# Relative-position bias tables: one matmul product for all eight heads, and one DMA that repeats its source rows

## The chip, the cores and the metric

The kernel runs on one core of one Trainium2 chip. The metric is the device time of one execution in microseconds (us). A core has TensorE (matrix products, PE in the profile), VectorE (DVE), ScalarE (ACT), GpSimd (POOL) and SyncE (SP), each with its own stream of instructions; they meet only through semaphores. SP, ACT and POOL also issue DMA transfers, which run on 16 shared DMA engines.

## The reference, cut to what matters

One layer of a hybrid model: an mLSTM branch and a sparse latent attention branch side by side, then a mixture of experts. Only the attention's relative bias is touched by the change:

```python
def _rel_bucket(dist):            # 32 buckets, exact up to 16, logarithmic up to 128
    n = jnp.maximum(dist, 0)
    ...
# rel_bias is [32 buckets, 8 heads]
l_sel = jnp.einsum('bqhr,bqkr->bqhk', ql, c_sel) + \
    rel_bias[_rel_bucket(t[None, :, None] - sel)].transpose(0, 1, 3, 2)
...
p = jax.nn.softmax(...)
```

The bias of a head depends on the distance between query and key alone. So one row of 656 numbers per head (`FX`), the bias at every distance, holds all that the attention needs; the row of each query is that row shifted by one place.

## The kernel before

The kernel is written by hand, engine by engine, with a semaphore for every hand-over. Input channels are projected in "units" of 256 columns (1024 KB of weights each): SP loads a unit into one of three slots of `raw` (`load(u)`, which waits until VectorE is done with the unit three back), ScalarE rounds it (`split_hi`, L646), VectorE forms the rest (`split_lo`, L1456), and TensorE runs three products per chunk (L1011 to L1013). Two split slots exist, so a split waits for the last use of the unit two back.

The bias goes in four steps. A constant `oneh` [32, 656] says which bucket each distance falls in. TensorE multiplies column h of `relb` [32 buckets, 8 heads], repeated 128 times, by `oneh` (`tables`, L1041): each of 128 partitions of `wide[h % 2]` in PSUM then holds the same 656 numbers of head h. ScalarE copies them to `ftab` [128, 4 buffers, 656] (`tables_out`, L648), and issues a DMA of 328 KB to `table_dram[h]`, shape (8, 128, 656) in DRAM (`tables_store`, L656). Much later SP reads `strips` back with a row step of 655 elements (L424), which shifts each partition's row by one place.

Heads go in pairs. Pair 0 is made before anything else. The others are written into the order of TensorE: `tables(2)` after the first unit's products, `tables(4)` after the second block of unit 1 (`B_QI + 1`), `tables(6)` after the small transposes L1110, then `channel_unit(2)` (two blocks, B_QA), `index_scores(0)`, `channel_unit(3)`, `index_scores(1)`, transposes of `c_tok`, and `conv_unit(4, 0)` to `conv_unit(7, 6)`.

`ftab` lies on the bytes of `v_ext`. For that reason GpSimd waits for all table stores before it writes the ones of `v_ext` (L544), which raises `const_done` to 3; and ScalarE's `conv_in(0)` (L750), which evacuates the first convolution block into `pre`, waits for `const_done` 3. `conv_unit(5, 2)` on TensorE waits for `conv_in(0)`, since it writes the same PSUM. VectorE, from `index_scores(0)` on, runs an order of its own: the score sum, rounds of top-k (L1545, L1546), and between them `split_lo` and `conv` (L1560, L1562).

Of the kernel before, what the change touches and what calls it, by code (L numbers as in the profile page):

```python
# [8 lines left out]
F32 = mybir.dt.float32  # L9
# [6 lines left out]
ACT = mybir.ActivationFunctionType  # L16
# [3 lines left out]
P = 128  # L20
# [9 lines left out]
AH, AD = 8, 64  # L30
# [3 lines left out]
BUCKETS, MAX_EXACT, MAX_DIST = 32, 16, 128  # L34
# [22 lines left out]
FX = STRIP + P - 1 + 1  # L57
# [27 lines left out]
def build(nc, a, onehot, router_const, entries, no_token, slot_numbers, out, h_dram, table_dram, h1_dram, list_dram, y_dram):  # L85
    w_in = a["w_in"][0].rearrange("(c p) n -> p c n", p=P)
    with ExitStack() as ctx:
        base = 16640

        def at(name, shape, dtype, kb):  # L90
            return nc.alloc_sbuf_tensor_at(name, shape, dtype, offset=base + int(kb * 1024))

        def sem(name):
            return ctx.enter_context(nc.semaphore(name))
# [7 lines left out]
        def little(name, shape, dtype=F32):  # L102
            nonlocal small_at
            n = int(np.prod(shape[1:])) * (2 if dtype in (BF16, F16) else 4)
            t = at(name, shape, dtype, small_at)
            small_at += -(-n // 32) * 32 / 1024
            assert small_at <= 62, small_at
            return t
# [34 lines left out]
        relb = little("relb", [BUCKETS, AH])  # L143
# [17 lines left out]
        A0 = 62.0  # L161
# [38 lines left out]
        o_lat = at("o_lat", [P, AH // 2, P], F32, A0 + 102.5)  # L200
        wuv = at("wuv", [P, AH, AD], F32, A0 + 118.5)
        h_aT = at("h_aT", [P, AH // 2, S], F32, A0 + 136.5)
        ftab = at("ftab", [P, 4, FX], F32, A0 + 51)
        oneh = at("oneh", [BUCKETS, FX], F32, A0 + 139.5)

        gates = [at(f"gate{i}", [P, S], F32, A0 + (69.5 + 2 * i if i < 12 else 108 + 2 * (i - 12))) for i in range(2 * KC)]
# [45 lines left out]
        wide = [ctx.enter_context(nc.psum_tensor(f"wide{i}", [P, 1024], F32)) for i in range(2)]  # L252
# [6 lines left out]

        names = """  # L260
            const_done vec_step act_step pool_step zero_done
            table_in wuk_loaded table_done table_out strips_loaded
            load_consts load_late
            var_ready rstd_ready xn_ready xt_done hi_x lo_x affine_m xm_ready shift_ready h_ready h_stored
            hi_ready lo_ready
# [8 lines left out]
            heads_hi heads_lo  # L274
            bm_done ba_done bm_ready y_ready y_hi y_lo
            z_part h_loaded  vm_ready
            late_consts z_added var1_ready rstd1_ready h1t_done h1t_used h1t_out h1_ready h1_stored gained
            router_done scores_ready chosen_ready  dest_ready  listed lists_loaded lists_ready
            m_hi_ready m_lo_ready m_used xe_done xe_hi_ready xe_lo_ready gate_ready hid_ready hd_done
            hd_hi_ready hd_lo_ready y_out passed pool_move all_scattered  # L280
# [2 lines left out]
        """.split()  # L283
        q = {n: sem(n) for n in names}
        x_loaded = [sem(f"x_loaded{i}") for i in range(TT + 1)]
        table_stored = [sem(f"table_stored{i}") for i in range(2)]
        gathered = [sem(f"gathered{i}") for i in range(2)]
        scattered = [sem(f"scattered{i}") for i in range(2)]
        m_loaded = [sem(f"m_loaded{i}") for i in range(MR)]
# [87 lines left out]
        def _(sp):  # L377
# [38 lines left out]
                load(u)  # L416

            sp.wait_ge(q["st_done"], MH)
            for stored in table_stored:
                sp.wait_ge(stored, 16 * AH // 2)  # L420
            for h in range(AH):
                src = bass.AP(tensor=table_dram.tensor, offset=table_dram.offset + h * P * FX + P - 1,
                              ap=[[FX - 1, P], [1, STRIP]])
# [68 lines left out]
        def _(pool):  # L492
# [46 lines left out]

            pool.wait_ge(q["h_stored"], 16 * TT)  # L540
            step(nc.gpsimd.memset(pre[:, :, 0:CONV - 1], 0.0))
            for stored in table_stored:
                pool.wait_ge(stored, 16 * AH // 2)
            nc.gpsimd.memset(v_ext[:, :, :, P:P + 1], 1.0).then_inc(q["const_done"], 1)  # L544
            pool.wait_ge(q["const_done"], 3)

# [92 lines left out]
        def _(act):  # L639
            step = Chain(act, q["act_step"])  # L640

            def split_hi(u):
                act.wait_ge(raw_loaded[u % RAW], load_total(u))
                if u >= SPL:
                    act.wait_ge(*last_use(u - SPL))
                nc.scalar.activation(w_hi[:, u % SPL, :], raw[:, u % RAW, :], ACT.Copy).then_inc(q["hi_ready"], 1)  # L646

            def tables_out(h0):  # L648

                for h in (h0, h0 + 1):  # L650
                    act.wait_ge(q["table_done"], h + 1)
                    if h >= 4:
                        act.wait_ge(table_stored[h % 2], 16 * (h // 2))
                    nc.scalar.activation(ftab[:, h % 4, :], wide[h % 2][:, 0:FX], ACT.Copy).then_inc(q["table_out"], 1)

            def tables_store(h0):  # L656

                for h in (h0, h0 + 1):
                    act.wait_ge(q["table_out"], h + 1)
                    act.dma_start(table_dram[h], ftab[:, h % 4, :]).then_inc(table_stored[h % 2], 16)  # L660

            tables_out(0)

            for i in range(TT):
                act.wait_ge(q["shift_ready"], i + 1)
# [16 lines left out]
            act.wait_ge(q["affine_m"], 1)  # L682
            nc.scalar.activation(hT_hi[:, :, 0:META], tmpM[:, :, :], ACT.Copy).then_inc(q["hi_x"], 1)
            split_hi(1)
            tables_store(0)

            act.wait_ge(q["block_done"], B_SMALL + 1)
            step(nc.scalar.activation(kidx2[0:64, :].rearrange("p (x y) -> p x y", x=2), both_halves(low[0][0:64, :]), ACT.Copy))
# [3 lines left out]
            act.wait_ge(q["kv_done"], 1)  # L692
            nc.scalar.activation(in_halves(cT[:, :]), both_halves(low[1][:, :]), ACT.Copy).then_inc(q["kv_out"], 1)
            act.wait_ge(q["load_late"], 16 * 10)
            tables_out(2)
            tables_store(2)

            step(nc.scalar.activation(rows[96:100, 0, :], smallT[96:100, :], ACT.Abs, bias=bif[96:100, 0:1]))
            step(nc.scalar.activation(rows[96:100, 0, :], rows[96:100, 0, :], ACT.Exp, scale=-1.0))
# [14 lines left out]
            def evac(b, dst, func=ACT.Copy):  # L714

                act.wait_ge(q["block_done"], b + 1)
                src = bank[b % 2][:, :]
                if len(dst.shape) == 3:
                    src = bank[b % 2][:, 0:dst.shape[1] * dst.shape[2]].rearrange("p (x y) -> p x y", x=dst.shape[1])
                elif len(dst.shape) == 4:  # L720
                    src = src.rearrange("p (x y z) -> p x y z", x=dst.shape[1], y=dst.shape[2])
                nc.scalar.activation(dst, src, func).then_inc(q["block_out"], 1)  # L722

            act.wait_ge(q["h_stored"], 16 * TT)
            evac(B_QI, qidxT[:, 0, :])
            tables_out(4)
            tables_store(4)
            evac(B_QI + 1, qidxT[:, 1, :])
            split_hi(3)
            tables_out(6)  # L730
            tables_store(6)

            def index_relu(n):

# [262 lines left out]
        def _(pe):  # L997
            def take(b):

                pe.wait_ge(q["block_out"], max(b - 1, 1))  # L1000
                return bank[b % 2]
# [13 lines left out]
            def by_channel(outp, u, m, lo, hi):  # L1015

                wh, wl = has(u)
                for k in range(KC):
                    mm = product(outp, (wh[:, k, m:m + P], wl[:, k, m:m + P]),
                                 (hT_hi[:, k, lo:hi], hT_lo[:, k, lo:hi]), k == 0, k == KC - 1)  # L1020
                return mm
# [16 lines left out]
                                 (wh[:, k, m:m + n], wl[:, k, m:m + n]), k == 0, k == KC - 1)  # L1038
                return mm

            def tables(h0):  # L1041

                for h in (h0, h0 + 1):
                    if h >= 2:
                        pe.wait_ge(q["table_out"], h - 1)
                    rb = relb[:, h:h + 1].to_broadcast([BUCKETS, P])
                    nc.tensor.matmul(wide[h % 2][:, 0:512], rb, oneh[:, 0:512], start=True, stop=True)
                    nc.tensor.matmul(wide[h % 2][:, 512:FX], rb, oneh[:, 512:FX], start=True, stop=True).then_inc(q["table_done"], 1)


            pe.wait_ge(q["table_in"], 32)
            tables(0)

            pe.wait_ge(q["table_out"], 2)
            pe.wait_ge(q["const_done"], 1)
            for i in range(TT):
                pe.wait_ge(q["xn_ready"], i + 1)
# [20 lines left out]
            def channel_unit(u, b):  # L1078
                for m in range(2):
                    by_channel(take(b + m)[:, :], u, m * P, META, T).then_inc(q["block_done"], 1)  # L1080
# [8 lines left out]
            def index_scores(n):  # L1089
# [6 lines left out]
                                          kidx2[lo:lo + 64, META:META + P * (n + 2)], start=True, stop=True)  # L1096
                mm.then_inc(q["idx_done"], 1)

            tables(2)
            by_channel(take(B_QI)[:, :], 1, 0, META, T).then_inc(q["block_done"], 1)  # L1100
            pe.wait_ge(q["kv_out"], 1)
            nc.tensor.transpose(bank[2][0:META, 160:160 + R], cT[:, 0:META], ident[:, :])
# [1 line left out]
                mm = nc.tensor.transpose(bank[3][:, i * R:(i + 1) * R], cT[:, META + i * P:META + (i + 1) * P], ident[:, :])  # L1104
            mm.then_inc(q["ckv_done"], 1)
            by_channel(take(B_QI + 1)[:, :], 1, P, META, T).then_inc(q["block_done"], 1)
            tables(4)
            pe.wait_ge(q["c_ready"], TT + 1)
            for i in range(TT):
                mm = nc.tensor.transpose(bank[2][:, 448 + 8 * i:456 + 8 * i], smallT[64:72, META + i * P:META + (i + 1) * P], ident[64:72, 64:72])  # L1110
            mm.then_inc(q["wt_done"], 1)
            tables(6)
            channel_unit(2, B_QA)
            pe.wait_ge(q["table_out"], AH)
            pe.wait_ge(q["block_out"], B_QI + 2)
            index_scores(0)
            channel_unit(3, B_QA + 2)
# [16 lines left out]
            for n in range(2):  # L1134
                by_token(bank[3][:, 256 * n:256 * (n + 1)], 8 + n, 0, 256, 0, P)
                for t2 in range(2):
                    o = take(B_V + 2 * n + t2)
# [18 lines left out]
            for h in range(AH):  # L1156
                lo = (h % 2) * 64
                nc.tensor.matmul(take(B_QLAT + h)[:, :], wukT[lo:lo + 64, h // 2, :], qaT[lo:lo + 64, h // 2, :],  # L1158
                                 start=True, stop=True).then_inc(q["block_done"], 1)
# [4 lines left out]
            for h in range(MH + 1):  # L1164
                if h < MH:
# [5 lines left out]
                    for j in range(TT):  # L1171
                        o = bank[5][:, :] if j == 0 else bank[6][:, 0:384] if j == 1 else bank[7][:, 0:256] if j == 2 else bank[7][:, 256:384]
# [5 lines left out]
                if h:  # L1178
                    g = h - 1
                    pe.wait_ge(q["w_ready"], h)  # L1180
                    for i in range(TT):
                        if i % 2 == 0:
                            o = take(B_NUM + 2 * g + i // 2)
# [51 lines left out]
            for n in range(2 * TT):  # L1235
# [5 lines left out]
                for i in range(4):  # L1241
                    h = 4 * (n % 2) + i
# [5 lines left out]
                for i in range(4):  # L1248
                    h = 4 * (n % 2) + i
                    o = take(B_PT + 4 * n + i)  # L1250
# [19 lines left out]
            for half in range(2):  # L1270
                for br in range(2):
# [4 lines left out]
                    for i in range(4):  # L1276
# [4 lines left out]
                        o = bank[4 + i if br == 0 else i][:, :]  # L1281
# [685 lines left out]
```

## Time and profile before

| | |
|---|---|
| median of 3 runs | 886.03 us (884.76 to 887.33) |
| profiled execution | 888.82 us |
| its span, first to last instruction | 887.1 us |
| PE, DVE, ACT, POOL busy | 89%, 67%, 49%, 12% of the span |
| mean granted TensorE clock | 0.951 of full speed |

All views come from one profiled execution. Times in them count from the start of the span. The profiled execution is 1.7 us longer than its span and 2.8 us longer than the median of the runs.

### The profile page before, as it was taken

To read this page: it belongs to the slowest core of one execution; us is meant where nothing else is said; L and a number is where in the kernel's file an instruction comes from. 1 tells how busy PE (TensorE), PEld (TensorE's weight loads), DVE (VectorE), ACT (ScalarE), POOL (GpSimd) and SP (SyncE) were. 2 spreads that over 40 slices of the span, in tenths; PEclk is the share of its full clock that TensorE was granted. 3 is DMA by queue.
4 is the path that set the end of the run, shared out by engine and by line. 5 is a ranking of instruction groups with operands and counts; after the bars stand their busy time and mean duration, and the time that the engine had idled before them with its cause. 6 is when DMAs were issued, how large, how long until landed. Compare 5 with 4: busy or idle time off the path is not lost.

```text
span 887.1 us, 10600 instructions
## 1 busy us (share of the span) xinstructions
PE 786.7 (89%) x3903; PEld 617.8 (70%) x3905; DVE 592.4 (67%) x793; ACT 430.9 (49%) x497; POOL 103.2 (12%) x115
## 2 busy tenths in 40 slices
PE   4499999999998999999999984799999999999920
PEld 2387898984676454688788873688888888888710
DVE  4805999793237654222356577799888988898838
ACT  5343343244532644422123121487778777877713
POOL 4630000000001000000000021211112111212012
PEclk9999999997999999999999985899999999999975
DMA  7644132400051300034323975499999999997143
GB/s 187 223 137 157 48 96 57 134 1 1 0 193 60 96 1 0 1 95 159 125 95 104 359 297 177 160 360 384 400 398 397 398 400 396 398 401 272 61 168 136
DMA packets 102644, 167.05 MB, mean 188 GB/s; under 512 B 18961, under 2 KB 39697, under 8 KB 102609
## 3 DMA queue, kind: packets, MB, share of 16 engines
q1 hardware_dynamic: 95024, 145.53, 46.3%
q0 software_dynamic: 4752, 13.11, 3.8%
q10 hardware_dynamic: 2832, 7.93, 2.3%
q8 instruction: 23, 0.38, 0.2%
q14 instruction: 13, 0.10, 0.0%
HBM read 153.38 MB, written 17.40 MB: 193 GB/s over the span
## 4 chain that ended last, share of the span: by engine, by line
PE 77%; DVE 11%; ACT 4%; issue 3%; DMA 2%; SPq 1%; POOL 1%; POOLq 0%; DVEq 0%; ACTq 0%
PE low L1011 14%; PE low L1012 14%; PE low L1013 14%; PE wide L1011 6%; PE wide L1013 6%; PE wide L1012 6%; PE wide L1365 2%; PE low L1188 1%; PE low L1260 1%; PE wide L1173 1%; ACT prob L844 1%; PE wide L1214 1%; PE low L1317 1%; PE low L1252 1%; PE low L1158 1%
## 5 line engine op out<-in xcount | busy, mean ns | idle before, releaser
L1731 DVE TENSOR_TENSOR m_lo<-m_raw,m_hi 128x2048 fp32r<-128x2048 f32 x95 | 214.9, 2290 | 28.4 <-ACT m_hi L890 25.4
L890 ACT ACTIVATE m_hi<-m_raw 128x2048 fp32r<-128x2048 f32 x95 | 179.1, 1917 | 25.6 <-PE low L1013 25.6
L1456 DVE TENSOR_TENSOR w_lo<-raw,w_hi 128x2048 fp32r<-128x2048 f32 x28 | 64.1, 2290 | 79.9 <-ACT w_hi L646 79.6
L1011 PE MATMUL low<-m_hi,xe_hi 128*128 128x512 f32 x256 | 103.7, 405 | 3.6 <-DVE xe_lo L1796 3.2
L1011 PE MATMUL low<-hT_hi,w_hi 128*128 128x512 f32 (+1 forms) x240 | 93.2, 388 | 10.7 <-issue 10.7
L1012 PE MATMUL low<-m_lo,xe_hi 128*128 128x512 f32 x256 | 100.4, 392 | 0.0
L1013 PE MATMUL low<-m_hi,xe_lo 128*128 128x512 f32 x256 | 100.4, 392 | 0.0
L1012 PE MATMUL low<-hT_lo,w_hi 128*128 128x512 f32 (+1 forms) x240 | 93.0, 387 | 0.0
L1013 PE MATMUL low<-hT_hi,w_lo 128*128 128x512 f32 (+1 forms) x240 | 92.3, 385 | 0.0
L646 ACT ACTIVATE w_hi<-raw 128x2048 fp32r<-128x2048 f32 x28 | 53.5, 1910 | 18.6 <-PE wide L1013 8.3
L1011 PEld LDWEIGHTS low<-hT_hi,w_hi 128*128 128x128 f32 x240 | 46.7, 195 | 20.9 <-issue 11.2
L1011 PEld LDWEIGHTS low<-m_hi,xe_hi 128*128 128x128 f32 x256 | 48.4, 189 | 17.4 <-DVE m_lo L1731 4.6
L1013 PEld LDWEIGHTS low<-m_hi,xe_lo 128*128 128x128 f32 x256 | 48.5, 189 | 10.5
L1012 PEld LDWEIGHTS low<-m_lo,xe_hi 128*128 128x128 f32 x256 | 48.6, 190 | 9.1
L1013 PEld LDWEIGHTS low<-hT_hi,w_lo 128*128 128x128 f32 x240 | 46.6, 194 | 9.0
L1012 PEld LDWEIGHTS low<-hT_lo,w_hi 128*128 128x128 f32 x240 | 46.5, 194 | 8.9
L1011 PE MATMUL wide<-m_hi,hd_hi 128*128 128x512 f32 x128 | 51.1, 399 | 1.6 <-DVE hd_lo L1805 1.6
L1013 PE MATMUL wide<-m_hi,hd_lo 128*128 128x512 f32 x128 | 50.0, 390 | 0.0
L1012 PE MATMUL wide<-m_lo,hd_hi 128*128 128x512 f32 x128 | 49.9, 390 | 0.0
L722 ACT ACTIVATE gate<-low 128x512 f32<-128x512 f32 x16 | 9.6, 598 | 66.2 <-PE low L1013 66.2
L1011 PE MATMUL wide<-hT_hi,w_hi 128*128 128x264 f32 x128 | 36.6, 286 | 3.3 <-ACT pre L750 1.2
L922 ACT ACTIVATE xe_hi<-wide 128x1024 fp32r<-128x1024 f32 x16 | 16.4, 1027 | 43.9 <-PE wide L1365 43.9
(337 smaller groups left out, 1524.7 us busy)
## 6 DMA issues: line engine op xcount, KB each, us to landing
m_raw<-in_w_gate SPq DMA_DIRECT2D x32, 1024.0 KB, 8.1
m_raw<-in_w_up SPq DMA_DIRECT2D x32, 1024.0 KB, 8.0
m_raw<-in_w_down SPq DMA_DIRECT2D x31, 1024.0 KB, 9.4
raw<-in_w_in SPq DMA_DIRECT2D x19, 1024.0 KB, 5.4
raw<-in_w_out SPq DMA_DIRECT2D x4, 1024.0 KB, 5.1
table_dram<-ftab ACTq DMA_DIRECT2D x8, 328.0 KB, 2.8
strips<-table_dram SPq DMA_DIRECT2D x8, 264.0 KB, 4.2
xn<-in_x SPq DMA_DIRECT2D x4, 512.0 KB, 5.2
```

The costliest lines, as they stand in the source:

```text
L646: nc.scalar.activation(w_hi[:, u % SPL, :], raw[:, u % RAW, :], ACT.Copy).then_inc(q["hi_ready"], 1)
L722: nc.scalar.activation(dst, src, func).then_inc(q["block_out"], 1)
L844: nc.scalar.activation(prob[:, h, 0:w], prob[:, h, 0:w], ACT.Exp, scale=-1.0, bias=nmax[:, h:h + 1], accum_out=psums[:, h:h + 1]).then_inc ...
L890: nc.scalar.activation(m_hi[n % MS][:, :], (m_spare if is_last(n, j) else m_raw[slot])[:, :], ACT.Copy).then_inc(q["m_hi_ready"], 1)
L922: nc.scalar.activation(xe_hi[:, :, :], wide[1][:, :].rearrange("p (c x) -> p c x", c=KC), ACT.Copy).then_inc(q["xe_hi_ready"], 1)
L1011: nc.tensor.matmul(outp, lh, rh, start=first, stop=False)
L1012: nc.tensor.matmul(outp, lh, rl, start=False, stop=False)
L1013: return nc.tensor.matmul(outp, ll, rh, start=False, stop=last)
L1158: nc.tensor.matmul(take(B_QLAT + h)[:, :], wukT[lo:lo + 64, h // 2, :], qaT[lo:lo + 64, h // 2, :], start=True, stop=True).then_inc(q["blo ...
L1365: mm = nc.tensor.transpose(wide[1][:, c * P:(c + 1) * P], xg[slot][:, c * P:(c + 1) * P], ident[:, :])
L1456: v.tensor_tensor(w_lo[:, u % SPL, :], raw[:, u % RAW, :], w_hi[:, u % SPL, :].bitcast(F32), ALU.subtract).then_inc(q["lo_ready"], 1)
L1731: v.tensor_tensor(m_lo[n % MS][:, :], (m_spare if is_last(n, j) else m_raw[n % MR])[:, :], m_hi[n % MS][:, :].bitcast(F32), ALU.subtract). ...
```

## The change

All eight bias rows come from one product: `relb` [32, 8] itself is the stationary operand, so that the result has eight rows, one for each head. ScalarE copies these eight rows once, into `ftab` [8, 656]. One DMA, issued by ScalarE after `split_hi(3)`, writes all of `table_dram`: its source repeats each of the eight rows 128 times with a step of zero. The three later pairs leave TensorE's order and the four `tables_out` and `tables_store` leave ScalarE's; two semaphores for the stores become one. `v_ext` still overlaps `ftab`, and the waits on the store stay on GpSimd and SP.

```diff
-        ftab = at("ftab", [P, 4, FX], F32, A0 + 51)
+        ftab = at("ftab", [AH, FX], F32, A0 + 51)
...
             sp.wait_ge(q["st_done"], MH)
-            for stored in table_stored:
-                sp.wait_ge(stored, 16 * AH // 2)
+            sp.wait_ge(q["table_stored"], 16)
...
             step(nc.gpsimd.memset(pre[:, :, 0:CONV - 1], 0.0))
-            for stored in table_stored:
-                pool.wait_ge(stored, 16 * AH // 2)
+            pool.wait_ge(q["table_stored"], 16)
             nc.gpsimd.memset(v_ext[:, :, :, P:P + 1], 1.0).then_inc(q["const_done"], 1)
...
-            tables_out(0)
+            act.wait_ge(q["table_done"], 1)
+            nc.scalar.activation(ftab[:, :], wide[0][0:AH, 0:FX], ACT.Copy).then_inc(q["table_out"], 1)
...
             split_hi(1)
-            tables_store(0)
...
             act.wait_ge(q["load_late"], 16 * 10)
-            tables_out(2)
-            tables_store(2)
...
             evac(B_QI, qidxT[:, 0, :])
-            tables_out(4)
-            tables_store(4)
             evac(B_QI + 1, qidxT[:, 1, :])
             split_hi(3)
-            tables_out(6)
-            tables_store(6)
+            act.wait_ge(q["table_out"], 1)
+            act.dma_start(table_dram, ftab[:, :].rearrange("h (o f) -> h o f", o=1).to_broadcast([AH, P, FX])).then_inc(q["table_stored"], 16)
...
             pe.wait_ge(q["table_in"], 32)
-            tables(0)
-
-            pe.wait_ge(q["table_out"], 2)
+            nc.tensor.matmul(wide[0][0:AH, 0:512], relb[:, :], oneh[:, 0:512], start=True, stop=True)
+            nc.tensor.matmul(wide[0][0:AH, 512:FX], relb[:, :], oneh[:, 512:FX], start=True, stop=True).then_inc(q["table_done"], 1)
+            pe.wait_ge(q["table_out"], 1)
...
-            tables(2)
             by_channel(take(B_QI)[:, :], 1, 0, META, T).then_inc(q["block_done"], 1)
...
-            tables(4)
             pe.wait_ge(q["c_ready"], TT + 1)
...
             mm.then_inc(q["wt_done"], 1)
-            tables(6)
             channel_unit(2, B_QA)
-            pe.wait_ge(q["table_out"], AH)
             pe.wait_ge(q["block_out"], B_QI + 2)
             index_scores(0)
```

## Rows read from the trace of the kernel before

**Rows 1.** The page: PE's share, and ScalarE's DMA queue (packets, MB, share).

```profile
PE 786.7 (89%) x3903; PEld 617.8 (70%) x3905; DVE 592.4 (67%) x793; ACT 430.9 (49%) x497; POOL 103.2 (12%) x115
q10 hardware_dynamic: 2832, 7.93, 2.3%
```

**Rows 2.** The chain that ended last (start, us, what), at the span's start.

```profile
4.58 1.00 SPq L384
5.62 5.07 SPq L390
...
13.16 4.86 DMA raw<-in_w_in
```

**Rows 3.** Busy time by stretch: stretch, length, engines, then PEclk, DMA share, GB/s.

```profile
40.59:45.99 5.40, 5.40 (x25) 5.40 (x25) 2.10 (x1) 0.00 (x0) 5.32 (x2) 1.00 0.25 100
46.11:54.57 8.46, 8.46 (x73) 8.46 (x71) 0.00 (x0) 1.82 (x3) 6.05 (x3) 1.00 0.33 119
54.78:57.18 2.40, 2.40 (x10) 1.28 (x9) 0.00 (x0) 1.33 (x2) 0.00 (x0) 1.00 0.95 315
57.18:62.86 5.68, 5.68 (x25) 4.52 (x25) 0.00 (x0) 4.01 (x5) 0.00 (x0) 1.00 0.65 216
...
69.08:74.04 4.96, 4.96 (x21) 2.65 (x20) 4.82 (x10) 2.77 (x4) 0.00 (x0) 0.92 0.62 178
74.04:80.50 6.46, 6.46 (x24) 5.19 (x24) 5.24 (x6) 2.50 (x3) 0.04 (x1) 0.80 0.61 235
```

**Rows 4.** The store of the tables: POOL's wait, the DMA view of 36 to 44 us.

```profile
80.46 0.14 POOL L544 MEMSET v_ext<- 128x20 f32 x1 [12.89 <-DMA table_dram<-ftab]
...
GB/s 430 389 430 389 471 410 103 0 0 0 0 0 0 0 105 394 394 420 394 368 420 394 420 53 0 0 471 430 389 451 410 410 62 0 0 0 0 0 0 0
...
table_dram<-ftab ACTq DMA_DIRECT2D x2, 328.0 KB, 2.5
```

**Rows 5.** The chain that ended last, from 114 us on.

```profile
114.84 0.30 issue
115.14 0.61 ACT pre L750
131.49 0.66 ACT kT L755
132.27 0.51 DVE cacc L1560
```

**Rows 6.** Timeline of PE: start, us, what, idle time before and its releaser.

```profile
40.59 0.56 PE L1011 MATMUL low<-hT_hi,w_hi 128*128 128x264 f32 x1 [10.69 <-issue]
...
115.80 0.39 PE L1011 MATMUL wide<-hT_hi,w_hi 128*128 128x264 f32 x1 [1.19 <-ACT pre L750]
...
140.35 0.36 PE L1011 MATMUL wide<-hT_hi,w_hi 128*128 128x264 f32 x1 [1.09 <-DVE w_lo L1456]
```

**Rows 7.** Timeline of DVE.

```profile
67.52 2.29 DVE L1456 TENSOR_TENSOR w_lo<-raw,w_hi 128x2048 fp32r<-128x2048 f32 x1 [1.46 <-ACT w_hi L646]
69.73 1.36 DVE L1505 SCALAR_TENSOR_TENSOR c_tok<-low,crs,kvg 128x128 f32<-128x128 f32 x5
...
88.18 0.35 DVE L1531 TENSOR_SCALAR score<-relu,widx 128x256 f32<-128x256 f32 x1 [8.73 <-ACT relu L740]
...
118.69 0.50 DVE L1560 TENSOR_SCALAR cacc<-pre,cw 128x528 f32<-128x528 f32 x1
```

**Rows 8.** Timeline of ACT and of its DMA queue (ACTq).

```profile
38.10 0.34 ACTq L660 DMA_DIRECT2D table_dram<-ftab  x1
38.30 1.89 ACT L646 ACTIVATE w_hi<-raw 128x2048 fp32r<-128x2048 f32 x1
...
102.10 1.94 ACT L646 ACTIVATE w_hi<-raw 128x2048 fp32r<-128x2048 f32 x1
```

**Rows 9.** SP's issues of the weight loads in the stretch of the store.

```profile
69.84 0.37 SPq L390 DMA_DIRECT2D raw<-in_w_in  x1
79.48 0.37 SPq L390 DMA_DIRECT2D raw<-in_w_in  x1
```

More of the change, by code:

```diff
@@ L261, in build @@
             const_done vec_step act_step pool_step zero_done
-            table_in wuk_loaded table_done table_out strips_loaded
+            table_in wuk_loaded table_done table_out table_stored strips_loaded
             load_consts load_late
@@ L276, in build @@
             z_part h_loaded  vm_ready
-            late_consts z_added var1_ready rstd1_ready h1t_done h1t_used h1t_out h1_ready h1_stored gained
+            late_consts z_added var1_ready rstd1_ready h1t_done h1t_used h1t_out h1_ready h1_stored
             router_done scores_ready chosen_ready  dest_ready  listed lists_loaded lists_ready
@@ L285, in build @@
         x_loaded = [sem(f"x_loaded{i}") for i in range(TT + 1)]
-        table_stored = [sem(f"table_stored{i}") for i in range(2)]
         gathered = [sem(f"gathered{i}") for i in range(2)]
@@ L646, in split_hi @@
                 nc.scalar.activation(w_hi[:, u % SPL, :], raw[:, u % RAW, :], ACT.Copy).then_inc(q["hi_ready"], 1)
[L648 to L660, printed above, removed]
-            tables_out(0)
+            act.wait_ge(q["table_done"], 1)
+            nc.scalar.activation(ftab[:, :], wide[0][0:AH, 0:FX], ACT.Copy).then_inc(q["table_out"], 1)
             for i in range(TT):
@@ L1039, in by_token @@
                 return mm
[L1041 to L1048, printed above, removed]
             pe.wait_ge(q["table_in"], 32)
-            tables(0)
-            pe.wait_ge(q["table_out"], 2)
+            nc.tensor.matmul(wide[0][0:AH, 0:512], relb[:, :], oneh[:, 0:512], start=True, stop=True)
+            nc.tensor.matmul(wide[0][0:AH, 512:FX], relb[:, :], oneh[:, 512:FX], start=True, stop=True).then_inc(q["table_done"], 1)
+            pe.wait_ge(q["table_out"], 1)
             pe.wait_ge(q["const_done"], 1)
```

## The prediction, made before the kernel was changed

> **What bounds the kernel now.** TensorE is busy 89% of the span and DVE 67% [rows 1], so I ask where TensorE's products for the tables lie on the chain that ended last. The first pair does not matter: at that time the chain runs through SP's issues and the first weight load, to 18 us [rows 2]. The other three pairs lie inside TensorE's unbroken run: `tables(2)` fills 2.40 us, `tables(4)` and `tables(6)` with the small transposes between them 4.96 us, and the block behind them takes 6.46 us where the same 24 products took 5.68 us earlier; the granted clock reads 0.92 and 0.80 of full speed in these two stretches and 1.00 in the earlier ones [rows 3]. So the tables cost more than their own time.
>
> Next I ask who waits for the store. POOL is released at 80.46 us [rows 4]; the next user of `const_done` 3, ScalarE's `conv_in(0)`, runs at 115.14 [rows 5]. In between lie 34.7 us of slack. `conv_in(0)` itself is on the chain: TensorE idles 1.19 us for it before `conv_unit(5, 2)` [rows 6], and the chain goes on from the convolution's first block through ScalarE's silu at 131.49 to DVE's `conv(2)` at 132.27 [rows 5]. DVE is only just behind: its `conv(0)` starts at 118.69, right behind its own work [rows 7].
>
> **What is taken away.** (a) `tables(2)`: 2.40 us of TensorE [rows 3]. (b) `tables(4)` and `tables(6)`: behind `B_QI + 1` TensorE must wait for `c_ready` anyway. It will arrive there at 69.08 − 2.40 = 66.7. `c_tok` ended at 69.73 + 1.36 = 71.1; it follows from `split_lo(2)` at 67.52 [rows 7], which follows from transposes that also come 2.40 us sooner, so it ends at 68.7 and TensorE goes on at about 68.7 + 0.3 for the four small transposes = 69.0. Before, `channel_unit(2)` began at 74.04, so it comes 5.0 us sooner. (c) If the clock stays up, its first block takes 5.68 instead of 6.46: 0.8 more. Sum 5.8 us. The bounds of (c): the new 2 us of idle could lower the clock itself, though the waits of 1.19 and 1.09 us further on did not break the pace; then the 0.8 is not won and up to 2.5 us (priced below) are lost. I take 0.8.
>
> ScalarE loses seven copies of tables and DVE nothing, but DVE's top-k begins when `index_scores(0)` is done. DVE waited 8.73 us for that, until 88.18 [rows 7]. So DVE, too, moves 5.8 us forward, and with it every split and load that hangs on it. Without anything else the whole kernel would end 5.8 us sooner.
>
> **What is added.** One DMA of 8 × 128 × 656 × 4 B = 2.687 MB, the bytes of the eight old ones together, in 1024 rows of 2624 B. Its issue stands behind `split_hi(3)`; ScalarE's sequencer runs ahead of its datapath (the old issue at 38.10 started before the `w_hi` copy at 38.30 that stands in front of it [rows 8]). The second block of unit 1 ends at 66.7, so the issue is at about 67.0. Old store: 336 KB landed in 2.5 us while the queues moved about 420 GB/s, 26.25 GB/s for each of 16 engines [rows 4]; 0.8 us is transfer and 1.7 us the fixed part. The queue's totals agree: 7.93 MB in 2.3% of 16 × 887.1 us is 24 GB/s per engine [rows 1].
>
> What no row shows is a store whose source lies in eight partitions. Old stores read 128 partitions, eight for each engine. The bounds: if only the number of engines counts and the eight rows use eight, 2.687 MB / (8 × 26.25) = 12.8 us (6.4 with sixteen); if the partitions count and eight of them give what eight gave before, one engine's worth, 2.687 / 26.25 = 102.4 us. Nothing in the rows excludes either. The arithmetic middle of 12.8 and 102.4 is 57.6 us; I take two engines' worth, 51.2 us, near to it. That is my choice, and the whole forecast hangs on it.
>
> The Trainium skill speaks against the change here. "SBUF — State Buffer", section "Door 1: The DMA port swizzle", says that DMA bandwidth goes by how many of 16 ports the partitions reach, that partitions 0 to 3 and 4 to 7 are one port each, and gives about 27 GB/s a port; "DMA: Bandwidth & Descriptors" says that the slowest dimension sets the number of engines, here eight. By the ports it would be an estimated 49.4 us of transfer, and the sum below 1.8 us less; by the engines alone it would be hidden. No trace here shows either yet.
>
> **The new wait.** Landing at 67.0 + 1.7 + 51.2 = 119.9. POOL's memset takes 0.14 [rows 4], a hand-over 0.30 [rows 5]: `conv_in(0)` can start at 120.3. All before it would be ready at 115.14 − 5.8 = 109.3, so ScalarE stands 11 us, and behind it TensorE: its only work up to there, `conv_unit(4, 0)` and four transposes, is done. `conv_in(0)` is 120.3 − 115.14 = 5.2 us later than before. DVE runs dry too, since `conv(0)` would be due at 118.69 − 5.8 = 112.9.
>
> After 10.69 us of idle time at 40.59 TensorE made 25 products in 5.40 us (0.216 each), and then 73 in 8.46 (0.116) [rows 3, 6]: a long idle costs 25 × (0.216 − 0.116) = 2.5 us at the restart. The new stall is as long, and TensorE is what `conv_in(2)`, `conv_in(3)`, `split_hi(7)` and the silu wait for in turn, so I charge all 2.5 us. ScalarE's chain from `conv_in(0)` to `conv(2)` has no slack before (DVE waits for the silu up to 132.27), and past it DVE and TensorE alternate: TensorE waits for `w_lo` at 140.35 [rows 6]. Nothing there gives the delay back.
>
> The weight loads run beside the store. SP issues them at 69.84 and 79.48 [rows 9], 2.4 us sooner each after the change. If each engine took one of its 64 weight rows for each row of the store, with 2624 B per 0.40 us on each of eight engines, a load would last 26 us. The first would land at 93.5, before its `w_hi` copy, 102.10 − 5.8 = 96.3 [rows 8]; the second at 119.5, just before its copy behind `conv_in(1)`. So they stay hidden, barely. In the other direction they may hold up the store: each gives eight engines 64 KB, 2.5 us, so up to 5 us. I take 0, since at 6.6 GB/s each the engines would not be the limit.
>
> **The sum.** The gain is already inside it, since the store starts early and lands when it lands: 5.2 + 2.5 = 7.7 us slower. The profiled execution took 888.82 us; it would be 896.5, its span 894.8. Against the median of the runs, 2.8 us lower, 886.03 + 7.7 = 893.7 us.
>
> **The rivals.**
> Rival A, the store is hidden. If the eight rows are read at three engines' worth or more (up to 34 us), it lands before 104 and nobody waits; the 5.8 us stand: 880.2 us. It decides from a landing before about 108.9. For it: in the rows an engine's rate is never seen to depend on partitions. Against: 12.8 us was only ever seen with sixteen times as many partitions. It is also the side of faster.
> Rival B, the two cancel. A landing between about 109 and 115 makes `conv_in(0)` as late as before, with or without the clock's 2.5: within 0.3% of 886.
> Rival C, far slower. One engine's worth, landing at 67.0 + 1.7 + 102.4 = 171.1: `conv_in(0)` at 171.5 is 56.4 late, with the clock 58.9: 945 us. Weight loads pulled along in it would make it no better.
> Rival D, the issue blocks. At the start SP stood 5.07 us at one issue behind two of 1024 small pieces each, of which the second took 1.00 [rows 2]. If the store's 128 rows per engine filled ScalarE's queue, ScalarE could not evacuate blocks from 75 us on; standing until about 110 costs 35 us: 921. Against: those two pieces put 128 on every engine and were still accepted.
>
> **How the numbers follow.** This kernel's measurement can tell about 0.3% (2.7 us) from no change. The forecast has 0.64, A 0.20, B 0.05, C 0.06, D 0.05. The forecast's own range: at 2.3 engines' worth 44.5 us, 6.7 less, about 887; with 5 us of contention and a rate a tenth lower, 5 + 5.7 more, 904. That is 0.64 alone; to hold 8 in 10 it must reach A as well: 879 to 904, which leaves out C, D and edges, some 0.14. Faster: A, 0.20. Same: B and a corner of the forecast, 0.08. Slower: 0.72.
>
> **What would show it.** TensorE has no table products past 10 us and starts `channel_unit(2)` near 69 [b]; its first block lasts 5.7 [c]; DVE's first `score` is near 82.4. The single store shows over 50 us from issue to landing, and POOL's memset of `v_ext` stands near 120 with a wait of more than 50. `conv_in(0)` (was 115.14) follows it, TensorE has 10 us of idle before `conv_unit(5, 2)`, and its products run at 0.22 for some 5 us. A store of under 40 us makes the forecast wrong and A right; TensorE at its full pace after the stall takes 2.5 us away; a weight unit that lands behind its `w_hi` copy adds a wait that I have priced at nothing.

## The result: 0.95% slower, and the profile after

The changed kernel took 893.07 us (median of 20 runs, 887.81 to 896.37), the kernel before on the same chips 885.39 us (20 runs, 880.79 to 888.62). The ratio is 1.0095, 95% interval [1.0074, 1.0116]. The profiled execution took 893.51 us, its span 891.8 us, at a mean granted clock of 0.944.

From the page of the changed kernel, PE's share and ScalarE's DMA queue (packets, MB, share of 16 engines' span); they answer to [rows 1]:

```profile
PE 777.9 (87%) x3877; PEld 612.6 (69%) x3877; DVE 590.1 (66%) x793; ACT 426.8 (48%) x490; POOL 102.3 (11%) x115
...
q10 hardware_dynamic: 2712, 7.93, 4.2%
```

TensorE has 8.8 us less to do and the kernel is longer. ScalarE's queue moved the same 7.93 MB and kept engines for 4.2% of the span instead of 2.3%. The store is the only thing in it that changed its form.

The timelines of ACT, POOL, PE and DVE around the store; they answer to [rows 4, 6, 7, 8]:

```profile
62.35 1.34 ACTq L710 DMA_DIRECT2D table_dram<-ftab  x1
97.06 1.92 ACT L643 ACTIVATE w_hi<-raw 128x2048 fp32r<-128x2048 f32 x1 [4.01 <-DMA raw<-in_w_in]
118.46 0.13 POOL L541 MEMSET v_ext<- 128x20 f32 x1 [57.82 <-DMA table_dram<-ftab]
118.63 1.11 ACT L729 ACTIVATE pre<-wide 128x528 f32<-128x528 f32 x2 [12.57 <-POOL v_ext L541]
119.34 0.50 DVE L1525 TENSOR_SCALAR cacc<-pre,cw 128x528 f32<-128x528 f32 x1 [9.88 <-ACT pre L729]
```

The store is issued at 62.35 and lands just ahead of 118.46, 56 us later. POOL has waited 57.82 us for it, ScalarE 12.57 us for POOL's memset, DVE 9.88 us for ScalarE. The chain of waits that ended last shows the same as one piece, which the profile names "unknown queue" and the timeline of POOL names the store:

```profile
60.64 57.71 another core or an unknown queue
118.46 0.14 POOL v_ext L541
118.63 0.62 ACT pre L729
119.29 0.59 PE wide L990
```

**Where the 4.7 us between the two spans lie.** The first product of unit 0 started at 37.36 (before: 40.59 [rows 6]). This moves from execution to execution without any change: 38.98 in another trace of the kernel before, 36.9 to 39.9 in the variants below. So I count from it. `conv_in(0)` came 118.63 − 37.36 = 81.27 us behind the first product, before 115.14 − 40.59 = 74.55 [rows 5, 6]: 6.7 us later. The next 18.46 us, to DVE's `conv(2)`, took 132.27 − 115.14 = 17.13 us before [rows 5]: 1.3 us more. Together 8.0 us, less the 3.2 us by which this execution began sooner: 4.8. Between the medians of the runs lie 7.7 us. The 20 runs of either kernel fall into two groups some 5 us apart (before 9 and 11 runs, medians 882.1 and 887.3; changed 10 and 10, medians 891.0 and 895.7), so that like for like the change costs 8.9 or 8.4 us.

### The profile page after: what moved, and what is told of

It is laid out like the page before. It is cut to its first block, busy times and chain, and to the rows that moved or that the text cites. A ratio compares the mean times of both kernels' runs of the same rounds, so it can differ in the third digit from the quotient of the medians.

```text
span 891.8 us, 10526 instructions
## 1 busy us (share of the span) xinstructions
PE 777.9 (87%) x3877; PEld 612.6 (69%) x3877; DVE 590.1 (66%) x793; ACT 426.8 (48%) x490; POOL 102.3 (11%) x115
## 3 DMA queue, kind: packets, MB, share of 16 engines
q10 hardware_dynamic: 2712, 7.93, 4.2%
## 4 chain that ended last, share of the span: by engine, by line
PE 71%; DVE 11%; another core or an unknown queue 6%; ACT 5%; issue 3%; DMA 2%; SPq 1%; POOL 1%; POOLq 0%; DVEq 0%; ACTq 0%
PE low L990 13%; PE low L992 13%; PE low L991 13%; PE wide L990 5%; PE wide L992 5%; PE wide L991 5%; PE wide L1330 2%; PE low L1153 1%; PE low L1225 1%; PE wide L1138 1%; ACT prob L823 1%; PE wide L1179 1%; PE low L1282 1%; PE low L1123 1%
```

## The experiments

All variants keep the single product and leave the three later table pairs out of TensorE's order. Those called "spread" widen the stationary operand, so that the result has more rows. In them the row of one head stands in several partitions.

**1. Which partitions hold the source.** The rival here was that the store is slow for another reason: its repeating source, its size, or its 128 descriptors on each of eight engines.

```diff
-        ftab = at("ftab", [AH, FX], F32, A0 + 51)
+        ftab = at("ftab", [AH * 16, FX], F32, A0 + 51)
+        relx = at("relx", [BUCKETS, AH * 16], F32, A0 + 142.25)
...
+            nc.scalar.activation(relx[:, :].rearrange("b (h o) -> b h o", o=16), relb[:, :].rearrange("b (h o) -> b h o", o=1).to_broadcast([BUCKETS, AH, 16]), ACT.Copy).then_inc(q["relx_ready"], 1)
...
-            act.dma_start(table_dram, ftab[:, :].rearrange("h (o f) -> h o f", o=1).to_broadcast([AH, P, FX])).then_inc(q["table_stored"], 16)
+            act.dma_start(table_dram.rearrange("h (j o) f -> (h j) o f", j=16), ftab[:, :].rearrange("h (o f) -> h o f", o=1).to_broadcast([AH * 16, P // 16, FX])).then_inc(q["table_stored"], 16)
...
```

That is the first, with 128 source rows, each repeated 8 times; the product and ScalarE's copy grow to 128 rows with it (not shown). 

> The same eight rows, but each head's row stands in 16 partitions (one product of 128 outputs), and the one DMA repeats each of 128 rows 8 times instead of each of 8 rows 128 times. Same bytes, same number of rows of 2624 B, same place of issue. If the eight source partitions make the store slow, it lands in under 15 us, GpSimd's memset of v_ext stands near 75 us, the wait before conv_in(0) is gone and the kernel is about 5 to 6 us faster than before the change (ratio 0.993 to 0.995), 13 to 14 us faster than the changed kernel. If a source that repeats with a step of zero is slow in itself, the store still takes over 40 us and the ratio stays near 1.009.

The second has 32 rows in `ftab`, of which every fourth is stored, 128 times each: eight rows as in the change, but four partitions apart (`ftab[0:32:4, :]`). 

> Each head's row stands in 4 partitions, and the one DMA reads every fourth of the 32: eight rows 128 times each, as in the changed kernel, but from partitions 0, 4, 8 to 28 instead of 0 to 7. Number of rows, repeats and outer sizes are those of the changed kernel. If neighbouring source partitions share a read rate, these eight are apart and the store runs two to four times faster, lands well before 109 us, and the ratio to before is near 0.994. If the eight engines that such a shape uses, or the repeats, set the rate, the store moves about 70 GB/s as in the changed kernel and the ratio stays near 1.009.

The third has two rows for each head in partitions 0 to 15, repeated 64 times: sixteen engines, but adjacent partitions. 

> Each head's row stands in 2 partitions; the one DMA repeats each of 16 rows 64 times, from partitions 0 to 15. By the number of partitions touched the store's own rate is about twice that of the changed kernel, 140 GB/s, some 20 us of transfer plus what the weight loads take, landing near 90 to 95, ahead of conv_in(0): ratio near 0.994. If only the number of engines counted, sixteen would give it about 400 GB/s and it would last 7 to 9 us.

The fourth stores eight rows sixteen partitions apart (`ftab[0:128:16, :]`), 128 times each. 

> A look at where source rows may stand: eight rows read from partitions 0, 16, 32 to 112. At stride 4 (0 to 28) the store took 19.5 us, eight engines at their full rate. If any eight partitions that are at least four apart are as good, it takes 19 to 20 us again; if partitions 32 apart share a rate as neighbours do, as the port table of the SBUF page says, these eight are four pairs and it takes 27 to 30 us.

The 70 and 140 GB/s in two of these expectations are what all queues together moved beside the change's store, and twice that; the store's own rate in the change is 50 GB/s (below).

POOL's memset in the four, in this order (spread over 128, eight rows four apart, sixteen adjacent, eight rows sixteen apart), from the timelines of POOL:

```profile
76.72 0.14 POOL L542 MEMSET v_ext<- 128x20 f32 x1 [14.20 <-DMA table_dram<-ftab]
```

```profile
82.80 0.14 POOL L542 MEMSET v_ext<- 128x20 f32 x1 [21.32 <-DMA table_dram<-ftab]
```

```profile
94.23 0.14 POOL L542 MEMSET v_ext<- 128x20 f32 x1 [30.69 <-DMA table_dram<-ftab]
```

```profile
94.83 0.14 POOL L542 MEMSET v_ext<- 128x20 f32 x1 [30.96 <-DMA table_dram<-ftab]
```

| source rows in partitions | engines | issue to landing | store's rate, steady | time of the kernel, ratio to before |
|---|---|---|---|---|
| 0 to 7 (the change) | 8 | 56 us | 50 GB/s | 893.07, 1.0095 [1.0074, 1.0116] |
| 0 to 15 | 16 | 28.9 us | 100 GB/s | 879.29, 0.9939 [0.9911, 0.9968] |
| 0, 16, ... 112 | 8 | 29 us | 100 GB/s | 880.62 (one run) |
| 0, 4, ... 28 | 8 | 19.5 us | 160 GB/s beside loads | 879.06, 0.9932 [0.9905, 0.9958] |
| all 128 | 16 | 12.4 us | 290 GB/s beside loads | 877.11, 0.9928 [0.9896, 0.9959] |

The profile doesn't name the engines of a DMA. The second column is read from the outermost size (8, or a multiple of 16), and the shares of 16 engines below agree with it: never half for eight, 92% for sixteen. The rates come from the view of the DMA queues: queue (q10 is ScalarE's, q1 SP's), packets, MB, share of 16 engines. First the changed kernel, 78 to 91 us:

```profile
q10 hardware_dynamic: 248, 0.65, 45.1%
q1 hardware_dynamic: 248, 0.25, 5.4%
```

Then "sixteen adjacent", 67 to 71 us and 71 to 76 us:

```profile
q10 hardware_dynamic: 154, 0.40, 91.7%
q1 hardware_dynamic: 17, 0.02, 1.2%
...
q10 hardware_dynamic: 192, 0.50, 92.1%
q1 hardware_dynamic: 191, 0.20, 10.9%
```

Then "eight rows sixteen apart", 71 to 76 us:

```profile
q10 hardware_dynamic: 191, 0.50, 40.4%
q1 hardware_dynamic: 192, 0.20, 10.9%
```

Last "eight rows four apart", 71 to 80 us:

```profile
q10 hardware_dynamic: 549, 1.44, 40.0%
q1 hardware_dynamic: 914, 0.92, 31.8%
```

The bytes, the repetition and the 128 descriptors on each engine are the same in the change, in "sixteen apart" and in "four apart", and a row of 2624 B keeps its engine for 0.451 × 16 × 13 us / 248 = 0.38 us, for 0.404 × 16 × 5 / 191 = 0.17 us, and for 0.400 × 16 × 9 / 549 = 0.105 us (25 GB/s, where an engine moved 26 in the old stores [rows 4]). Sixteen adjacent partitions employ sixteen engines and each row takes 0.921 × 16 × 5 / 192 = 0.38 us again. So neither size nor repetition nor the number of engines sets the rate. Four adjacent partitions together get what one engine can draw, 25 GB/s: two such groups give 50, four give 100.

Sixteen apart there are no neighbours, and still the eight rows get no more than four groups' worth. The table of "SBUF — State Buffer", section "Door 1: The DMA port swizzle", of the Trainium skill names them: partitions 0 and 32 are on one port, and so are 16 and 48, 64 and 96, 80 and 112, which makes four ports of these eight. By that table the five sources reach 2, 4, 4, 8 and 16 ports. The traces agree: 50 GB/s over two ports and 100 over four are 25 GB/s a port, a little under the 27 that the Trainium skill gives there. With 8 and 16 ports (20 and 18 GB/s a port, beside loads) no trace shows the ports as the limit.

With a quick store the gain is there. In "spread over 128" `conv_in(0)` stands 107.87 − 38.74 = 69.1 us behind the first product, 5.4 us sooner than before, and the kernel is 0.72% faster than before.

**2. The wait, or the load?** `ftab` gets bytes of its own, and POOL no longer waits for the store.

```diff
-        ftab = at("ftab", [AH, FX], F32, A0 + 51)
+        ftab = at("ftab", [AH, FX], F32, A0 + 142.125)
...
-            pool.wait_ge(q["table_stored"], 16)
             nc.gpsimd.memset(v_ext[:, :, :, P:P + 1], 1.0).then_inc(q["const_done"], 1)
```

> The changed kernel with ftab on bytes of its own, so that GpSimd writes the ones of v_ext without waiting for the store; the store itself is unchanged and as slow. If the stall of conv_in(0) behind the store is the whole loss, the kernel is 5 to 6 us faster than before (ratio 0.993 to 0.995). If the store costs mainly through the weight loads that it slows down, at least half of the loss stays: ratio over 1.002.

Measured: 887.34 us (12 runs), ratio 1.0028 [1.0005, 1.005]. The timeline of ACT:

```profile
109.45 1.11 ACT L728 ACTIVATE pre<-wide 128x528 f32<-128x528 f32 x2
122.54 1.91 ACT L642 ACTIVATE w_hi<-raw 128x2048 fp32r<-128x2048 f32 x1 [11.97 <-DMA raw<-in_w_in]
```

and that of "spread over 128" at the same place:

```profile
107.87 1.11 ACT L732 ACTIVATE pre<-wide 128x528 f32<-128x528 f32 x2
108.85 1.93 ACT L644 ACTIVATE w_hi<-raw 128x2048 fp32r<-128x2048 f32 x1
```

`conv_in(0)` is free of the store, at 109.45, and the kernel is still no faster than before. The next thing in ScalarE's order, the `w_hi` copy of unit 6, waits 11.97 us for its weight load. The load was issued while the store was under way, and its rows take turns with the store's: in the changed kernel 248 packets of the one and 248 of the other in 13 us (the view of the queues above), 209 and 208 from 104 to 115 us. There the two loads of this stretch landed 34 and 46 us after their issue (62.91 and 72.56), the second queued behind the first; the median load took 6.4 us.

How the loss divides is read at DVE's `conv(2)`, which lies behind both waits. From the timelines of DVE, "own bytes" first, then "spread over 128":

```profile
131.69 0.49 DVE L1524 TENSOR_SCALAR cacc<-pre,cw 128x528 f32<-128x528 f32 x1
```

```profile
124.99 0.49 DVE L1529 TENSOR_SCALAR cacc<-pre,cw 128x528 f32<-128x528 f32 x1 [0.75 <-ACT kT L737]
```

Counted from the first product (39.91, 38.74 and, in the change, 37.36) this is 91.8, 86.3 and 99.7 us: of the 13.5 us that the slow store costs there, 8.0 go with POOL's wait and 5.5 stay through the load. In the medians the same three kernels lie 16.7 parts in a thousand apart, of which 6.7 go and 10 stay; with intervals of 2 to 3 parts on either side of each ratio they don't divide the loss more closely, and what of the 10 lies elsewhere is not shown. In the changed kernel the two waits end within a microsecond of each other (118.46 and 118.9), so taking one alone gives only part of the loss.

**3. The same slow store, early.** The issue stands behind `split_hi(1)`, 26 us sooner, where nobody waits for it until `conv_in(0)`.

```diff
             split_hi(1)
+            act.wait_ge(q["table_out"], 1)
+            act.dma_start(table_dram, ftab[:, :].rearrange("h (o f) -> h o f", o=1).to_broadcast([AH, P, FX])).then_inc(q["table_stored"], 16)
...
             split_hi(3)
-            act.wait_ge(q["table_out"], 1)
-            act.dma_start(table_dram, ftab[:, :].rearrange("h (o f) -> h o f", o=1).to_broadcast([AH, P, FX])).then_inc(q["table_stored"], 16)
```

> The changed kernel, its store from eight neighbouring partitions unchanged, but issued some 27 us sooner, behind split_hi(1) where the first two old stores stood. At 48 GB/s it lands near 92 us, before conv_in(0) is due (about 107) and before the second weight load that it held up is issued behind a free queue. If the loss is only that store and held-up loads end too late, it is gone: ratio to before 0.993 to 0.995 like the spread store. If a slow store costs wherever it stands, because the loads of its own stretch (units 4 and 5, the stores of h) are held up, the ratio stays over 1.000.

Measured: 899.85 us (6 runs, 896.97 to 903.0), ratio 1.0172 [1.0135, 1.0208], worse than the change. The timelines of ACT, PE and POOL:

```profile
36.53 1.30 ACTq L670 DMA_DIRECT2D table_dram<-ftab  x1
78.88 0.28 ACT L691 ACTIVATE md<-low 128x128 f32<-128x128 f32 x1 [22.13 <-DMA h_dram<-xn]
86.42 0.59 PE L1077 MATMUL low<-ident,smallT 8*128 8x8 f32 x4 [22.08 <-DVE c_tok L1470]
96.77 0.13 POOL L541 MEMSET v_ext<- 128x20 f32 x1 [13.93 <-DMA table_dram<-ftab]
```

The store took 60 us and was out of `conv_in(0)`'s way (128.55). What it met earlier was other traffic: the last of SP's stores of `h_dram`, which ScalarE needs at once, took 28.0 us to land where it took 3.2 in the change, and ScalarE and TensorE each stood 22 us. The weight load issued next to it took 45.7 us. A store through two engines' worth of bandwidth has to take its 56 to 60 us somewhere, and in both places tried it held up the transfers of SP's beside it.

**4. The clock at `channel_unit(2)`.** In the change, TensorE waits 2.01 us for `c_tok`, and then its products run at half pace. The variant is "spread over 128" with the first block of unit 2, which needs nothing of `c_tok`, ahead of that wait.

```diff
+            by_channel(take(B_QA)[:, :], 2, 0, META, T).then_inc(q["block_done"], 1)
             pe.wait_ge(q["c_ready"], TT + 1)
...
-            channel_unit(2, B_QA)
+            by_channel(take(B_QA + 1)[:, :], 2, P, META, T).then_inc(q["block_done"], 1)
```

> The kernel with the row of each head in 16 partitions, and in TensorE's order the first block of unit 2 moved ahead of the wait for c_ready and of the four small transposes. If the 2.0 us of idle at that wait and the half pace behind it (0.43 instead of 0.235 us a product for about 3.5 us) are real losses on the path, it is 2 to 3.5 us faster than the same kernel without the move: ratio to before 0.989 to 0.991. If DVE's order bounds the stretch behind it, the ratio stays at 0.993.

Measured: 877.08 us (6 runs), ratio 0.9902 [0.9867, 0.9937]. TensorE's timeline of "spread over 128", and under it that of this variant:

```profile
66.10 0.41 PE L1081 MATMUL low<-ident,smallT 8*128 8x8 f32 x4 [2.01 <-DVE c_tok L1474]
66.44 0.64 PE L993 MATMUL low<-hT_hi,w_hi 128*128 128x512 f32 x1
66.87 0.63 PE L994 MATMUL low<-hT_lo,w_hi 128*128 128x512 f32 x1
```

```profile
65.36 0.47 PE L993 MATMUL low<-hT_hi,w_hi 128*128 128x512 f32 x1 [0.82 <-DVE w_lo L1426]
65.66 0.39 PE L994 MATMUL low<-hT_lo,w_hi 128*128 128x512 f32 x1
65.89 0.39 PE L995 MATMUL low<-hT_hi,w_lo 128*128 128x512 f32 x1
```

Starts lie 0.43 us apart behind a wait of 2.01 us and 0.23 us apart behind one of 0.82 us. All seven traces with the wait of 2.0 us (that of the change and six of the variants') have such a slow stretch of some 3 to 4 us behind it, and neither of the two traces with the moved block has one there. `conv_in(0)` comes 66.2 us behind the first product instead of 69.1. Whether that reaches the end is a question of 3 us, so both were run again beside each other:

> The kernel of e1_spread128 once more, beside e10 on one chip. By both theories 877 us, 0.990 to 0.994 of the kernel before, conv_in(0) about 69.1 us behind the first product.

> The kernel of e6_products_first once more, directly beside e9. If the 3.0 us that unit 2's first block won at full pace reach the end: 3 us (3.4 in a thousand) under e9, about 874. If they are given back later, by a stretch of the latent products at half clock: within 1.5 us of e9. In both cases conv_in(0) comes about 66.2 us behind the first product.

Measured on one chip: "spread over 128" 878.62 us (6 runs, 875.62 to 881.57), ratio 0.9913 [0.9885, 0.9942]; with the first block ahead 880.04 us (8 runs, 878.08 to 883.78), ratio 0.994 [0.9916, 0.9964]. The intervals overlap and the second is not the faster. `conv_in(0)` was again sooner, 66.8 against 69.1 us behind the first product. The gain is given back at the latent products (L1127 and L1128), 94 us later. Timelines of PE in these two runs, first the spread, then the other:

```profile
199.92 1.61 PE L1127 MATMUL low<-qaT,wukT 64*128 64x512 f32 x4 [1.16 <-ACT q_lat L788]
201.72 1.61 PE L1127 MATMUL low<-qaT,wukT 64*128 64x512 f32 x4 [0.20 <-ACT q_lat L788]
203.53 1.61 PE L1127 MATMUL low<-qaT,wukT 64*128 64x512 f32 x4 [0.20 <-ACT q_lat L788]
```

```profile
199.87 7.84 PE L1128 MATMUL low<-qaT,wukT 64*128 64x512 f32 x12 [1.16 <-ACT q_lat L788]
```

The same twelve products end at 205.1 in the one and at 207.7 in the other, both behind an idle time of 1.16 us, and what follows stays slow for some microseconds more. By stretch (the last columns are the granted clock, the DMA share and GB/s), first the spread:

```profile
200.00:210.00 10.00, 9.60 (x27) 4.12 (x28) 2.80 (x5) 7.60 (x15) 0.00 (x0) 1.00 0.01 2
```

```profile
200.00:210.00 10.00, 10.00 (x15) 3.08 (x16) 2.31 (x5) 5.17 (x8) 0.00 (x0) 0.53 0.00 0
210.00:220.00 10.00, 10.00 (x32) 6.07 (x30) 2.65 (x5) 4.99 (x9) 0.00 (x0) 0.79 0.01 2
```

DVE's `hn` starts 223.8 and 223.9 us behind the first product in the two traces of "spread over 128", and 226.4 and 227.3 in the two of the variant. What was won ahead, 2.3 to 3.0 us, is more than lost there. It is not the last word either: from `hn` to the end of the span the variant's two traces take 611.6 and 611.7 us and those of "spread over 128" 614.5 both times, so that the spans end level, 838.0 and 839.0 against 838.4 and 838.3 us behind the first product. These 2.9 us lie among the experts (DVE's `m_lo` runs for 308 us from its first start to its last in the variant and for 311 in the other); what causes them was not looked for.

**5. The kernel before, once more,** for what two traces of one kernel differ by. 

> The kernel before once more, for a second trace of it: how far the first product's start (40.6 us in the first trace) moves from run to run. If the changed kernels' earlier starts (37.1 to 39.9 us) are chance, this one can start anywhere between 37 and 41; if they come from the change, it starts at 40 or later again.

Measured: one run of 882.3 us, span 880.6, which is 6.5 us under that of the trace in the rows above. Its windows, and then those of the first trace of before over the second of them:

```profile
210.00:220.00 10.00, 9.80 (x31) 4.97 (x32) 1.66 (x5) 8.28 (x15) 0.00 (x0) 1.00 0.01 2
220.00:230.00 10.00, 10.00 (x40) 5.98 (x38) 2.97 (x7) 6.54 (x12) 0.00 (x0) 1.00 0.00 0
```

```profile
210.00:220.00 10.00, 10.00 (x15) 2.62 (x12) 2.01 (x5) 5.04 (x8) 0.00 (x0) 0.50 0.01 2
220.00:230.00 10.00, 10.00 (x34) 6.36 (x32) 2.20 (x4) 4.81 (x9) 0.00 (x0) 0.83 0.00 0
```

The same stretch of the same code runs at half clock in one execution and at full clock in the other. `hn` starts 229.9 us behind the first product in the quick one and 235.1 in the slow one: 5.2 us. That is more than half of what the change costs, and about what separates the two groups of runs of each kernel, so a single trace of each kernel doesn't tell the change from this, and the comparison rests on medians. Ahead of that stretch the two agree within 0.7 us: `conv_in(0)` comes 74.55 and 75.2 us behind the first product.

## Why the prediction came out right, step by step

**Table products taken away, right.** DVE's first `score` came 79.00 − 37.36 = 41.6 us behind the first product, 47.6 before [rows 6, 7]. That is 6.0 us sooner where 5.8 were forecast, but not by the forecast's terms alone, as the next step shows. In "spread over 128" `conv_in(0)` showed the gain without the store: 5.4 us against the first trace of before, 6.1 against the second.

**(c), the clock stays up: wrong.** I took 0.8 us for it, and named the 2 us of idle time as what could undo it. It did:

```profile
64.23 0.59 PE L1077 MATMUL low<-ident,smallT 8*128 8x8 f32 x4 [2.01 <-DVE c_tok L1470]
64.75 0.80 PE L990 MATMUL low<-hT_hi,w_hi 128*128 128x512 f32 x1
65.34 0.63 PE L991 MATMUL low<-hT_lo,w_hi 128*128 128x512 f32 x1
```

These are lines of PE's timeline of the changed kernel. Thirteen products fill the 4.0 us from 64.75, where 17 did in the variant without the idle time, at granted clocks of 0.64 and 1.00. The first block of 24 products took 7.0 us, not 5.68, and so 0.5 us longer than before instead of 0.8 shorter. Experiment 4 points to the idle time as the cause. The gain was nevertheless full size, so more than 0.8 us came from elsewhere: `channel_unit(2)` began 64.75 − 37.36 = 27.4 us behind the first product, before 33.5 [rows 3, 6], 6.1 us sooner where 5.0 were forecast. About 1 us of that lies in unit 0's first 5.40 us, in which this trace made 34 products and the trace of before 25 [rows 3]. The second trace of before (experiment 5) made 33, so that part belongs to the execution and not to the change.

**The store's rate, right, by luck.** "Two engines' worth" was to take 51.2 + 1.7 us; it took 56 us in all, at a steady 50 GB/s or 1.9 engines' worth. In the prediction this was the middle between 12.8 and 102.4 us, near which two engines' worth lay, and no row spoke for it. What sets the rate, groups of adjacent partitions, was no term of the sum. The port table of the Trainium skill, which stood beside the sum as an estimate of 49.4 us, is what the four variants bear out. Landing was forecast at 119.9 and was 118.3. The two errors are opposite: the issue was 4.7 us sooner (62.35 for 67.0), 3.2 of it because this execution began sooner, and the transfer 3 us longer.

**The weight loads on the store, right at nothing.** With sixteen adjacent the store moved 0.40 MB in 4 us with hardly a load beside it and 0.50 MB in 5 us with as many packets of the load as of its own: 100 GB/s both times.

**The store on the weight loads: right in mechanism, wrong in what it is worth.** One row for one row held exactly. By 64 rows of 0.38 us and as many weight rows of 0.054 × 16 × 13 / 248 = 0.045 us a load alone takes 27 us, where 26 were forecast. From issue to landing the first was forecast at 26 us and took 34, of which 7 are not taken apart; the second, queued behind it, was forecast at 42 (77.1 to 119.5) and took 46. "Hidden, barely" was wrong for the first load (ScalarE waits 4.01 us at 97.06 for it) and hollow for the second. It landed at 118.9, beside the store, so it was hidden only behind the very wait that I charged. Experiment 2 priced it at 5.5 of the 13.5 us up to `conv(2)` once that wait is gone; the prediction had put it at nothing. Whoever had fixed the kernel by the prediction's account, giving `ftab` its own bytes, would have won 6.7 of 16.7 parts in a thousand and wondered about the rest.

**The new wait, right.** Predicted 5.2 us later for `conv_in(0)` and measured 6.7 us, counted from the first product. DVE ran dry as forecast.

**The restart at half pace: right in kind, half the size.** The term was 2.5 us. PE's timeline after the stall shows starts 0.22 us apart, and by windows (then the same code in the trace of before):

```profile
118.30:125.00 6.70, 5.71 (x36) 5.71 (x37) 5.45 (x9) 2.91 (x3) 0.13 (x1) 0.71 0.56 200
119.29:124.69 5.40, 5.40 (x33) 5.40 (x34) 5.14 (x8) 2.25 (x2) 0.00 (x0) 0.73 0.50 177
```

```profile
115.80:121.20 5.40, 5.40 (x44) 5.40 (x45) 5.12 (x11) 2.24 (x2) 0.00 (x0) 1.00 0.02 3
```

In 5.40 us TensorE made 33 products, where it made 44 before and I had counted with 25. The half pace lasted 3.0 us, and the delay to `conv(2)` was 1.3 us. The row that I took the price from is the slow end of a range: over unit 0's first 5.40 us the twelve traces have from 25 to 34 products. That row [rows 3] also gives a granted clock of 1.00 while its products start 0.22 us apart; there the slow start shows in the starts and not in the clock's column, and whether it is the same thing as the one behind the stall (0.50 from 118.30 to 121.30) is not shown.

**The rivals.** A (hidden) is what "spread over 128" does, 877.11 us against 880.2 forecast for it. B needed a landing before 115, and it was 118.3. C and D didn't happen: ScalarE's issue took 1.34 us, and 128 descriptors for each of eight engines were taken without standing.

The terms add up as 6.7 + 1.3 = 8.0 us for 5.2 + 2.5 = 7.7, with the median 7.7 us over that of before. The path is the one that was forecast. Its size is luck in two ways: the store's rate was a choice between bounds eight times apart, and a wait 1.5 us too short and a restart 1.2 us too long cancel.

## What to carry to other kernels

A DMA whose source stands in a few adjacent partitions is slow by where it stands, not by its bytes: copy the source to partitions spread over the whole range before repeating it (here, a stationary operand of 128 columns instead of 8, which cost 0.2 us on TensorE and a copy of 0.3 us on ScalarE at the start). A slow transfer also slows each transfer that shares its engines, row for row, so ask not only who waits for it but which loads run beside it. When two waits end together, take away both before judging what either costs.

## What the runs showed of the hardware

- Stores from partitions 0 to 7, 0 to 15, eight of 16 apart and eight of 4 apart ran at a steady 50, 100, 100 and (beside loads) 160 GB/s, with the same bytes. Sixteen engines gave no more than eight where they drew on as many ports.
- Where both queues had work on the same engines, they moved as many packets of the one as of the other (248 to 248, 209 to 208), though a row of the store kept its engine 0.38 us and a row of the load 0.045; 1024 KB loads took 34 and 46 us beside the store in place of 6.4.
- Behind 2.01 us of idle time TensorE's products ran at half clock for some 3 to 4 us (seven traces of seven), and behind 0.82 us at full clock (two of two). Behind 1.16 us, at the latent products, both were seen: 1.61 us for four products or 7.84 us for twelve, in different executions of kernels that differ nowhere near. What decides it there stays open. Four of the traces made for this study ran this stretch at full clock and eight had half clock in it; that the variant with its first block ahead fell on the half in both of its traces may be chance or cause. Three of that variant's first six runs took 874.3 to 875.4 us at a mean granted clock of 0.958 to 0.960, the other three, the traced one among them, 878.8 to 879.3 us at 0.952.
